# The compress key/value group first in layer two, its weight chunks used one by one

## The reference

```python
h = rms_norm(x, g_mix)
(q, k_c, v_c, k_s, v_s, k_w, v_w, g_logit,
 q_l, k_l, v_l, a_l, r_l) = jnp.split(h @ w_in, split_points(), axis=-1)

def compress(u, pe, w1, w2):
    blk = u[:, tok] + pe[None, None, :, None, :]
    blk = blk.transpose(0, 1, 3, 2, 4).reshape(B, n_cmp, HKV, -1)
    return (jax.nn.silu(blk @ w1) @ w2).transpose(0, 2, 1, 3)

kc = rms_norm(compress(k_cmp, pe_k, w_ck1, w_ck2), g_kc)
vc = compress(v_cmp, pe_v, w_cv1, w_cv2)
```

## Time and profile before

| | |
|---|---|
| time, median of 3 runs | 1780.81 us (1778.14 to 1782.61) |
| profiled execution | 1778.34 us, span 1776.3 us |
| TensorE / VectorE / ScalarE busy | 94% / 61% / 44% |
| mean granted TensorE clock | 0.981 of full |
| chain that ended last | TensorE 81%, VectorE 12%, issue 3%, ScalarE 2% |
| mean DMA rate | 170 GB/s |

### The profile page before, as it was taken

The page is one execution under the profiler, slowest core; times in us unless marked ns, Lnnn a source line. Parts: engine busy times, 40 slices in busy tenths (PEclk is TensorE's granted clock), DMA queues, the critical chain, the costliest instruction groups (busy, mean ns, idle before and its releaser), DMA issues.

```text
span 1776.3 us, 21774 instructions
## 1 busy us (share of the span) xinstructions
PE 1678.1 (94%) x7925; PEld 1381.0 (78%) x7925; DVE 1083.2 (61%) x1534; ACT 776.2 (44%) x1017; POOL 5.9 (0%) x25
## 2 busy tenths in 40 slices
PE   6999898998899899898999899999999999999998
PEld 5878677787675797787887788888878888888787
DVE  3699996667752576787565564444445444444443
ACT  3433465534431355434465464444433444444332
POOL 0000000000000000000000000000000000000000
PEclk8999999998999899999999999999999999999999
DMA  8554442554457253333654355555555555555553
GB/s 300 202 178 127 149 146 77 187 196 149 143 166 239 74 170 118 119 95 143 237 176 156 119 166 191 189 189 189 189 188 190 190 192 190 189 189 189 186 190 118
DMA packets 159479, 301.42 MB, mean 170 GB/s; under 512 B 5430, under 2 KB 24699, under 8 KB 158634
## 3 DMA queue, kind: packets, MB, share of 16 engines
q1 hardware_dynamic: 159402, 300.39, 50.8%
HBM read 298.27 MB, written 2.10 MB: 169 GB/s over the span
## 4 chain that ended last, share of the span: by engine, by line
PE 81%; DVE 12%; issue 3%; ACT 2%; DMA 1%; SPq 0%; DVEq 0%; ACTq 0%
PE ps_g L344 24%; PE ps_g L346 24%; PE ps_g L345 24%; DVE cT L1726 3%; DVE lo L363 3%; PE ps_m L276 2%; PE ps_m L932 1%; ACT hi L355 1%; DMA raw<-in_w_in_dram 1%; PE ps_m L1046 0%; PE ps_m L988 0%; PE ps_m L835 0%; PE ps_m L915 0%; DVE x L1898 0%; PE ps_m L996 0%
## 5 line engine op out<-in xcount | busy, mean ns | idle before, releaser
L363 DVE TENSOR_TENSOR lo<-raw,hi 128x1024 fp32r<-128x1024 f32 (+3 forms) x552 | 655.3, 1190 | 560.3 <-ACT hi L355 553.3
L355 ACT CAST hi<-raw 128x1024 fp32r<-128x1024 f32 (+3 forms) x552 | 563.8, 1024 | 809.2 <-PE ps_g L346 755.5
L344 PE MATMUL ps_g<-hi,aH 128*128 128x512 f32 (+3 forms) x1696 | 666.7, 393 | 26.0 <-DVE lo L363 20.3
L345 PE MATMUL ps_g<-lo,aH 128*128 128x512 f32 (+3 forms) x1696 | 652.9, 385 | 0.0
L346 PE MATMUL ps_g<-hi,aL 128*128 128x512 f32 (+3 forms) x1696 | 652.7, 385 | 0.0
L344 PEld LDWEIGHTS ps_g<-hi,aH 128*128 128x128 f32 x1696 | 325.5, 192 | 90.1 <-issue 30.2
L346 PEld LDWEIGHTS ps_g<-hi,aL 128*128 128x128 f32 x1696 | 324.9, 192 | 63.1
L345 PEld LDWEIGHTS ps_g<-lo,aH 128*128 128x128 f32 x1696 | 325.6, 192 | 59.2 <-issue 0.5
L344 PE MATMUL ps_g<-hi,guH 128*128 128x512 f32 x352 | 137.1, 390 | 0.0
L346 PE MATMUL ps_g<-hi,guL 128*128 128x512 f32 x352 | 137.0, 389 | 0.0
L345 PE MATMUL ps_g<-lo,guH 128*128 128x512 f32 x352 | 136.9, 389 | 0.0
(11 more groups left out here) (342 smaller groups left out, 1135.2 us busy)
## 6 DMA issues: line engine op xcount, KB each, us to landing
raw<-in_w_gu_dram SPq DMA_DIRECT2D x88, 1024.0 KB, 5.0
raw<-in_w_in_dram SPq DMA_DIRECT2D x76, 1024.0 KB, 5.2
raw<-in_w_down_dram SPq DMA_DIRECT2D x44, 1024.0 KB, 5.1
raw<-in_w_out_dram SPq DMA_DIRECT2D x32, 1024.0 KB, 5.1
raw<-in_w_ck_dram SPq DMA_DIRECT2D x8, 1024.0 KB, 5.3
raw<-in_w_cv_dram SPq DMA_DIRECT2D x8, 1024.0 KB, 5.5
raw<-in_w_in_dram SPq DMA_DIRECT2D x12, 512.0 KB, 3.7
raw<-in_w_cq_dram SPq DMA_DIRECT2D x4, 1024.0 KB, 5.5
```

Of the source, the lines that this page charges most:

```text
L344: pe.matmul(dst, xh, wh, start=first, stop=False)
L345: pe.matmul(dst, xh, wl, start=False, stop=False)
L355: act.copy(step_view(hi, s), raw_view(s)).then_inc(s_hi, 1)
L363: dve.tensor_tensor(step_view(lo, s), raw_view(s), step_view(hi, s).bitcast(F32), ALU.subtract).then_inc(s_lo, 1)
```

## The change

The group order becomes `ncmp`, `nq0`, `nq1`, `nslc`, `nwin`. The pair of units on the compress rows comes after step 2 of `nq0`, the third step after the first group. `direct` handles one chunk instead of four; a table `compress_after` names the eight steps behind which one chunk is multiplied, and the list of chunks takes each compress chunk in just behind the group chunk of that step. The query units after step 4 of `ncmp` go to step 3 of `nslc`. On VectorE the compress rows are taken out first, then `kp` is made, and the two `q_rows` follow. No arithmetic is added or left out.

```diff
--- before.py
+++ after.py
@@ -91,7 +91,7 @@
         group(name, w_in, col, n)
     for j in range(4):
         group(f"wo{j}", w_out, NG * j, NG)
-    for name, col, n in (("nq0", 0, 512), ("nq1", 512, 512), ("ncmp", 1024, 512), ("nslc", 1536, 512),
+    for name, col, n in (("ncmp", 1024, 512), ("nq0", 0, 512), ("nq1", 512, 512), ("nslc", 1536, 512),
...
@@ -117,6 +117,10 @@
     G = {g["name"]: g for g in groups}
 
 
+    compress_after = [("nq0", 5), ("nq1", 0), ("nq1", 2), ("nq1", 5),
+                      ("nq1", 7), ("nslc", 2), ("nslc", 4), ("nslc", 7)]
+    compress_src = [a[w][0].rearrange("(k p) n -> p k n", p=P)[:, 8 * c:8 * c + 8, :]
+                    for w in ("w_ck1_2", "w_cv1_2") for c in range(4)]
     chunks = []
     for g in groups:
         for c in range(g["kt"] // CHUNK):
@@ -124,12 +128,9 @@
                 :, g["k0"] + CHUNK * c:g["k0"] + CHUNK * (c + 1), g["col"]:g["col"] + g["n"]]
             chunks.append(dict(src=src, n=g["n"], k=CHUNK, step=g["s0"] + 2 * c, group=g))
             g.setdefault("c0", len(chunks) - 1)
-        if g["name"] == "nslc":
-            for w in ("w_ck1_2", "w_cv1_2"):
-                for c in range(4):
-                    src = a[w][0].rearrange("(k p) n -> p k n", p=P)[:, 8 * c:8 * c + 8, :]
-                    chunks.append(dict(src=src, n=256, k=8, step=None, group=None,
-                                       direct=sum(x["step"] is None for x in chunks)))
+            for i, (name, j) in enumerate(compress_after):
+                if name == g["name"] and j // 2 == c:
+                    chunks.append(dict(src=compress_src[i], n=256, k=8, step=None, group=None, direct=i))
...
             def nq_T(h):
-                rows_T([nq[:, t, hh, :] for hh in (h, h + 1) for t in range(TT)], 1 + h // 4)
-
-            def direct(i):
-                if i == 0:
+                rows_T([nq[:, t, hh, :] for hh in (h, h + 1) for t in range(TT)], 2 + h // 4)
+
+            def direct(n):
+                i, c = divmod(n, 4)
+                if n == 0:
                     pe.wait_ge(s_xl, built("h", KT))
-                pe.wait_ge(s_kp, i + 1)
-                for c in range(4):
-                    n = direct_chunks[4 * i + c]
-                    wait_raw(pe, n)
-                    for l in range(8):
-                        last = pe.matmul(ps_m[3][0:2 * NCMP, i * T:(i + 1) * T],
-                                         kp[:, i, 8 * c + l].rearrange("p k n -> p (k n)"),
-                                         raw[:, n % NRAW, l * T:(l + 1) * T], start=(c == 0 and l == 0),
-                                         stop=(c == 3 and l == 7))
-                    last.then_inc(s_direct, 1)
+                if c == 0:
+                    pe.wait_ge(s_kp, i + 1)
+                chunk = direct_chunks[n]
+                wait_raw(pe, chunk)
+                for l in range(8):
+                    last = pe.matmul(ps_m[3][0:2 * NCMP, i * T:(i + 1) * T],
+                                     kp[:, i, 8 * c + l].rearrange("p k n -> p (k n)"),
+                                     raw[:, chunk % NRAW, l * T:(l + 1) * T], start=(c == 0 and l == 0),
+                                     stop=(c == 3 and l == 7))
+                last.then_inc(s_direct, 1)
 
@@ -1067,22 +1069,21 @@
             for g in groups[15:28]:
                 for j in range(g["ns"]):
                     gemm(pe, g, j, A(aH), A(aL),
-                         (lambda j: pe.wait_ge(s_xl, built("h", 2 * j + 2))) if g["name"] == "nq0" else None)
+                         (lambda j: pe.wait_ge(s_xl, built("h", 2 * j + 2))) if g["name"] == "ncmp" else None)
                     here = (g["name"], j)
-                    if g["name"] == "nq0" and j < 4:
+                    if g["name"] == "ncmp" and j < 4:
                         h_T([j + 4])
+                    if here == ("nq0", 2):
+                        stg_heads(0, 1)
+                        stg_heads(2, 1)
+                    if here in compress_after:
+                        direct(compress_after.index(here))
                     if here == ("nq1", 4):
                         nq_T(0)
                         nq_T(2)
-                    if here == ("ncmp", 4):
+                    if here == ("nslc", 3):
                         nq_T(4)
                         nq_T(6)
-                    if here == ("nslc", 2):
-                        stg_heads(0, 3)
-                        stg_heads(2, 3)
-                    if here == ("nslc", 7):
-                        direct(0)
-                        direct(1)
                     if here == ("nwin", 1):
                         stg_heads(0, 4)
@@ -1449,23 +1450,23 @@
                 for j in range(g["ns"]):
                     split_hi(act, g["s0"] + j + LEAD)
                     here = (g["name"], j)
-                    if g["name"] == "nq0" and j < 4:
+                    if g["name"] == "ncmp" and j < 4:
                         h_hi([j + 4])
-                    if here == ("nq0", 7):
+                    if here == ("ncmp", 7):
                         row_squares()
+                    if here == ("nq0", 3):
+                        heads2(kcT, 0, None)
+                        heads2(vcT, 0, None)
                     if here == ("nq1", 1):
                         root(ss_q[:, 0])
                     if here == ("nq1", 5):
                         heads2(nqT, 0, colq)
                         heads2(nqT, 2, colq)
-                    if here == ("ncmp", 1):
+                    if here == ("nslc", 1):
                         root(ss_q[:, 1])
-                    if here == ("ncmp", 5):
+                    if here == ("nslc", 4):
                         heads2(nqT, 4, colq)
                         heads2(nqT, 6, colq)
-                    if here == ("nslc", 3):
-                        heads2(kcT, 0, None)
-                        heads2(vcT, 0, None)
                     if here == ("nwin", 0):
                         root(ss_k[:, 0])
...
@@ -1970,17 +1971,14 @@
                 dve.tensor_tensor(rows, rows, sums.unsqueeze(3).to_broadcast([P, TT, KVH, DK]),
                                   ALU.mult).then_inc(s_t2s, 1)
 
-            q_rows(0)
-            keep_up(G["ncmp"]["s0"])
-            q_rows(1)
-            keep_up(G["nslc"]["s0"])
+            keep_up(G["nq0"]["s0"])
             evac_rows("ncmp", lambda t: stg2[:, t, :])
             dve.memset(hidTv[:], 0.0).then_inc(s_c2v, 1)
             dve.memset(vc_bd[:], 0.0)
             dve.memset(pc[:], 0.0).then_inc(s_t2s, 1)
 
-            keep_up(G["nslc"]["s0"] + 4)
-            dve.wait_ge(s_t2c, 6)
+            keep_up(G["nq0"]["s0"] + 4)
+            dve.wait_ge(s_t2c, 2)
...
@@ -1989,6 +1987,10 @@
                             src[:, kv, 16 * h:16 * h + 16 * NCMP].rearrange("p (n b) -> p b n", b=16),
                             cols[:, pe0 + 16 * h:pe0 + 16 * h + 16].unsqueeze(2).to_broadcast([P, 16, NCMP]), ALU.add)
                 last.then_inc(s_kp, 1)
+            keep_up(G["nq1"]["s0"])
+            q_rows(0)
+            keep_up(G["nslc"]["s0"])
+            q_rows(1)
             keep_up(G["nwin"]["s0"])
             kv_rows(0, "nslc", vs)
@@ -1997,7 +1999,7 @@
             keep_up(G["nwin"]["s0"] + 4)
             dve.wait_ge(s_c2, 1)
             link(dve.tensor_copy(kcn[:], ps_m[1][0:2 * NCMP, 0:P]))
-            dve.wait_ge(s_t2s, 3)
+            dve.wait_ge(s_t2s, 1)
             for kv in range(KVH):
```

More of the change, by code:

```diff
@@ L1921, in _ @@
             for q in range(4):
-                keep_up(nq0 + 4 + q)
+                keep_up(first + 4 + q)
                 layer_norm_gain(q)
```

4 lines of the change are left out of this document (2 added, 2 removed).

## The result

| | kernel before | changed kernel |
|---|---|---|
| device time, median | 1780.79 us (1778.14 to 1784.01, 12 runs) | 1783.58 us (1780.94 to 1785.76, 12 runs) |
| ratio to before | | 1.0017, 95% interval 1.0009 to 1.0024 |
| profiled execution | 1778.34 us, span 1776.3 us | 1784.15 us, span 1782.3 us |

The change costs 2.8 us in the medians. That is inside the 0.3% counted as no change, but the interval leaves out 1: with twelve runs it is slightly slower, and not the +0.25 us of the sum.

The account below looks back on a forecast made before the run. TensorE, busy 94% of the span, was taken to bound the kernel. The terms 5.2 −2.25 −2.35 −1.75 +1.4 +0 = +0.25 us gave 1781.1 us, called no change, with a range from 1776 to 1786.5.

Parts of the forecast that it names:

- (a): Behind step 10, TensorE meets the moved compress pair and waits for its rows; step 11 starts later: +5.2 us.
- (b): The compress pair leaves its old place, where it held TensorE from 524.64 to 526.89: −2.25 us.
- (c, d): Window group: TensorE's wait shrinks to 0.6 us, −2.35 us, and the slow matmuls behind it go, −1.75 us.
- (d): Slow matmuls behind the window group's wait go: −1.75 us, or 0 if the low clock has another cause.
- (e): Compress matmuls in eight places, seven more than before, 0.2 us of switching each: +1.4 us, bounds 0 and +2.1.
- (f): Clock after the first wait: low stretch again a little over 6 us, taken as 0; bounds −1.3 and +1.9.
- costed at nothing: Compress operands, query root and transposes, and transfers were all expected in time for TensorE, adding no wait.
- The tightest is the chunk of steps 18 and 19: Among transfers, this chunk was expected ready after 7.5 us, TensorE reaching it after 14.4: margin 6.9 us.
- late chunks: Rival: compress chunks or operands come late and the compress matmuls wait in small amounts; +3, 1784; chance 0.09.
- interleaving pays: Rival: lead for VectorE and ScalarE also removes the 3.40 us wait behind the window group; −8.2, 1773; chance 0.08.
- the clock: Rival: clock stays low from the first wait into the first compress matmuls, slow window stretch stays; +3.9 us; chance 0.17.

Follow-up runs that it names:

- experiment 1: Changed kernel with the first query pair's transposes and copies one step later; 1780.78 us, ratio 0.9997.
- experiment 2: Changed kernel with the fifth compress chunk queued behind the weight chunk of steps 24 and 25, its matmuls one step later; 1784.09 us, ratio 1.0011.
- experiment 5: Changed kernel's group order, but all eight compress chunks multiplied in one batch behind step 7 of the selected group; 1785.39 us, ratio 1.0022.
- experiment 7: Kernel before, with weights of steps 11 to 13 rounded and subtracted ahead of the row squares and the first query pair one step later; 1776.9 us, ratio 0.9976.
- experiment 8: Kernel before with the root's wait filled by weight preparation and the first query pair two steps later; 1771.38 us, ratio 0.9945.
- experiment 6: Changed kernel with the root's wait filled by weight preparation, compress pair behind step 12, first compress chunk and query pair one step later; 1769.98 us, ratio 0.9942.
- experiment 3: Changed kernel with the compress pair released by the evacuation of its rows, not by the last memset; 1785.1 us, ratio 1.0017.
- experiment 4: Changed kernel with the first query pair one step later and the compress pair released by its rows' evacuation; 1779.92 us, ratio 0.9989.
- experiment 9: Experiment 6 with the window keys' transposes one step later; 1768.49 us, ratio 0.9926.

## Why the prediction was right, and where it was not

The forecast of no change and the range held, but the sum left out a term larger than its result: in the profile +3.7 us of waiting and slow matmuls at the query pair, to which +2.2 for +1.4, −3.6 for −4.1 and −1.26 for 0 add little. That the time still fell among those called no change, 2.8 us up where 0.25 was forecast, is in part luck: the bounds of the sum did not contain this term.

(a) Right: 476.15 forecast, 476.19 measured, +5.40 for +5.2. The wait is 9.36 us long and not 8 to 9, because TensorE came to it earlier; in experiments 1, 2 and 5, whose first step ran at low clock, it is 8.45. (b) Right. (c, d) Right in the profile, 0.5 us less than forecast. The wait of 0.64 us was forecast as 0.6. For (d), experiments 5 and 7 have since shown a wait of 2.63 and 2.59 us without a low clock and experiment 8 one of 2.61 us with it, so the 1.75 us need not be there in every run of the kernel before; the median may hold less of it.

(e) Mis-sized: +2.2 for +1.4. A visit takes 3.57 us from start to next start (28.56 for eight, 27.74 for the batch), and the steps behind it 0.2 us more (three steps 8.39 us where 8.19 are three undisturbed ones). I had counted 0.2 us a visit from the two ends of the batch; both together are 0.3.

(f) Mis-sized: −1.26 for 0, the favourable end of what I had bounded.

The failed step is in what was costed at nothing: "The root of the query rows and their transposes keep 3 us or more" and "The tightest is the chunk of steps 18 and 19". The root did keep its margin. The transposes did not, since the copy between the two units stands behind hi 24 in ScalarE's list, and hi 24 behind a transfer. I had looked for the chunk with the shortest distance to the step that needs it on TensorE, and there the margin of 6.9 us covered the lateness as I wrote. But a chunk is first needed by ScalarE, three steps ahead, and whatever ScalarE does next inherits the delay. The chunk of steps 24 and 25 was held up behind a compress chunk whose buffer a visit was still reading. (Of two chunks issued together I had put the later one 5 us late; it landed 2.2 us after the time of the first, and even that was enough.) Experiments 1 and 2 took this wait away from two sides; the first also took away the slowdown. It is a case of my rival "late chunks" in its cause (compress chunks hold up the queue), but not in its place: no visit ever waited.

The rival *interleaving pays* fails where it was to decide: the 3.40 us wait is unchanged. VectorE and ScalarE did get work beside the visits, but TensorE is busy on both sides: against the one batch it saved 2.0 us of waiting in the window group and paid 2.2 us for switching. Experiment 8 against 6 shows no difference in medians either. The Trainium skill (Perfetto Trace Analysis, Optimization Strategy) says that interleaving may help where the most-contended engine changes over time. Here TensorE was the busiest in both stretches, and the split brought no net gain. The rival *the clock* fails too: the matmuls were fast again before the first visit, the visits took 3.57 us from the first on, and the clock was 1.00 in the window group.

What I had seen and not valued is the size of the first wait. It cost the kernel before 5.62 us and 2.9 us of slow matmuls; the change lengthened it, and the versions with it filled are 0.55 and 0.58% faster than the kernel before in either order (experiments 8 and 6).

Open: why the 2.25 us of experiment 3, half of experiment 2 and the 3.26 us between experiment 5 and the changed kernel do not appear in the medians (they are there in the stretch from the root to the hidden rows), and how often the compress scores run at low clock (6.7 us in the profiles of the changed kernel and of experiments 2, 3 and 5 to 8, 3.8 to 4.2 in those of the kernel before and of experiments 1, 4 and 9).

## What to carry to other kernels

When a change moves transfers in a queue, follow each late chunk to its first reader and then down that engine's list: what waits on TensorE may be a small copy behind it. Where the critical engine waits for a long chain of others, look for engines that idle at the head of that chain, and let them prepare the next steps first; here that was worth more than reordering the groups. And when a kernel's own runs spread as far as the edit is worth, compare profiles over the stretch that the edit touches as well as the medians. Before a stretch without VectorE work is interleaved, ask whether TensorE ever waits in it.

## What the runs showed of the hardware

- A low granted clock does not follow a wait of a given length every time. At the same place, 2.65 us of waiting and 0.72 behind it in the kernel before, 2.61 us and 0.69 in experiment 8, but 2.63 and 2.59 us and 1.00 in experiments 5 and 7.
- The same first step of layer two took 2.84 us at clock 1.00 in one profile and 5.10 us at 0.52 in another, in kernels that are the same up to there.
- Of two transfers of 1 MB issued 0.4 us apart the first landed 5.4 us and the second 7.6 us after its issue; in experiment 2, with the two exchanged, 5.1 and 7.6. The median of the compress chunks before was 5.3.
- Changing between the weight stream of a step and the compress matmuls and back costs 0.3 us: a visit takes 3.57 us where the batch has 3.47, and the steps behind it 0.2 us more.
